# Second mixer: the low parts of its 32 weight tiles subtracted on VectorE instead of GpSimd

## The reference

```python
z = rmsnorm(x) @ w_in + b_in         # conv_a, conv_gate, q, k, v, o, i, f
u = conv_a * sigmoid(conv_gate)
u = silu(layernorm(causal_depthwise_conv(u, conv_w, conv_b)))      # 31 taps, 512 channels
qk = silu(causal_depthwise_conv([q, k], qk_conv_w, qk_conv_b))     # 4 taps
h = mlstm_chunkwise(q, k, v, i, f)                                 # 4 heads of 128
hm = groupnorm(sigmoid(o) * h) * mlstm_norm_g
x = x + [u, hm] @ w_out
```

## Time and profile before

| what | us |
|---|---|
| runs | 2023.34, 2024.51, 2026.22 |
| median | 2024.51 |
| profiled execution, span from first to last instruction | 2015.6 |
| median above that span | 8.9 |
| second mixer, first tile to end of tile 31 | 1182 to 1459 |
| expert stage | about 1493 to 1990 |

### The profile page before, as it was taken

One profiled execution on the slowest core, in us unless ns is written; L12 is line 12 of the kernel. 1 busy time (PEld: TensorE's weight loads), 2 busy tenths in 40 slices (PEclk: granted clock), 3 DMA queues, 4 the chain that ended last, 5 costly groups with the idle time before them and its releaser, 6 DMA issues.

```text
span 2015.6 us, 27480 instructions
## 1 busy us (share of the span) xinstructions
PE 1816.0 (90%) x9716; PEld 1274.7 (63%) x9716; DVE 852.1 (42%) x1244; ACT 436.7 (22%) x809; POOL 992.8 (49%) x536
## 2 busy tenths in 40 slices
PE   5999999999999799999999979998968988869783
PEld 4888888887777577888888747765743333323331
DVE  5444434320253567544443389777341111111114
ACT  3111100100244432111110053552321111111112
POOL 5888887777544378888887623321211111101001
PEclk8999999999999999999999989989979988989886
DMA  3333372433211123333333212210589999999995
GB/s 128 94 96 102 94 273 94 143 95 95 72 56 52 41 84 94 94 94 97 101 107 99 77 54 73 65 61 21 206 311 357 378 404 406 413 415 407 410 398 205
DMA packets 56977, 346.00 MB, mean 172 GB/s; under 512 B 8474, under 2 KB 8858, under 8 KB 44896
## 3 DMA queue, kind: packets, MB, share of 16 engines
q1 hardware_dynamic: 44640, 315.12, 42.7%
q10 hardware_dynamic: 7968, 19.46, 2.6%
q0 software_dynamic: 4320, 10.78, 1.5%
HBM read 475.06 MB, written 19.66 MB: 245 GB/s over the span
## 4 chain that ended last, share of the span: by engine, by line
PE 71%; DMA 14%; DVE 10%; ACT 3%; issue 1%; POOL 1%; SPq 0%; DVEq 0%; ACTq 0%; POOLq 0%
PE bank L460 31%; PE bank L431 12%; DMA big<-w_up_in 10%; PE bank L1821 7%; PE bank L1320 4%; PE bank L694 4%; PE bank L1839 2%; DVE big L1046 2%; PE bank L479 2%; PE bank L1434 2%; DMA ring<-w_down_in 1%; PE bank L1847 1%; DMA state<-w_down_in 1%; PE bank L612 1%; PE bank L672 1%
## 5 line engine op out<-in xcount | busy, mean ns | idle before, releaser
L277 POOL TENSOR_TENSOR weights_hi_parts<-ring,ones 128x1024 fp32r<-128x1024 f32 (+1 forms) x176 | 356.6, 2026 | 293.8 <-PE bank L460 130.2
L279 POOL TENSOR_TENSOR ring_parts<-ring,weights_hi_parts 128x1024 fp32r<-128x1024 f32 (+1 forms) x176 | 474.0, 2693 | 13.8
L460 PE MATMUL bank<-attention_buffers_parts,weights_hi_parts 128*128 128x512 f32 x832 | 328.1, 394 | 22.6 <-POOL ring_parts L279 17.9
L460 PE MATMUL bank<-state_parts,weights_hi_parts 128*128 128x512 f32 x832 | 325.7, 391 | 0.0
L460 PE MATMUL bank<-attention_buffers_parts,ring_parts 128*128 128x512 f32 x832 | 325.4, 391 | 0.0
L1821 PE MATMUL bank<-big,work 128*32 128x512 f32 x1440 | 227.6, 676 | 51.3 <-DMA big<-w_up_in 51.2
L431 PE MATMUL bank<-big_parts,weights_hi_parts 128*128 128x512 f32 x704 | 216.9, 389 | 1.2 <-POOL ring_parts L279 1.2
L460 PEld LDWEIGHTS bank<-attention_buffers_parts,weights_hi_parts 128*128 128x128 f32 x832 | 157.4, 189 | 59.1 <-POOL ring_parts L279 17.9
L1921 POOL TENSOR_TENSOR small<-small 128x1 f32<-128x1 f32 x51 | 9.7, 190 | 371.5 <-DVE small L1744 371.5
L866 POOL TENSOR_TENSOR ring_parts<-ring,weights_hi_parts 128x1024 fp32r<-128x1024 f32 x32 | 80.7, 2524 | 220.2 <-ACT weights_hi_parts L863 220.2
L460 PEld LDWEIGHTS bank<-state_parts,weights_hi_parts 128*128 128x128 f32 x832 | 157.5, 189 | 32.9 <-issue 0.8
(11 more groups left out here) (386 smaller groups left out, 2830.2 us busy)
## 6 DMA issues: line engine op xcount, KB each, us to landing
big<-w_up_in SPq DMA_DIRECT2D x54, 2048.0 KB
ring<-wdense_in SPq DMA_DIRECT2D x176, 512.0 KB, 3.6
state<-w_down_in SPq DMA_DIRECT2D x37, 2048.0 KB
big<-w_gate_in SPq DMA_DIRECT2D x36, 2048.0 KB
attention_buffers<-w_gate_in SPq DMA_DIRECT2D x18, 2048.0 KB
ring<-w_down_in SPq DMA_DIRECT2D x18, 2048.0 KB
ring<-wff_in SPq DMA_DIRECT2D x32, 704.0 KB, 4.1
y_rows<-big ACTq DMA_DIRECT2D x1, 8192.0 KB, 28.1
```

Source lines behind the costliest of these rows:

```text
L277: po.tensor_tensor(hi, raw, ones[:, 0:1].to_broadcast([128, words]), ALU.mult).then_inc(PO.sem, 1)
L279: po.tensor_tensor(lo, raw, hi.bitcast(F32), ALU.subtract) \
L460: m = pe.matmul(out, x, y_, start=j + n == 0, stop=j == len(pairs) - 1 and n == len(ts) - 1)
```

## The change

The low part of every tile of the second mixer is subtracted on VectorE, behind the same wait for the high part, and the planner's clock of VectorE is moved on by 1.15 for it. Nothing is left on GpSimd in the mixer.

```diff
             AC.wait(ring_freed[n - 2] if n >= 2 else before_ring[n + 2])
             hi_made[n] = AC.step(ac.activation(hi, raw, ACT.Copy))
             est("ac", 1.15)
-            PO.wait(hi_made[n])
-            lo_made[n] = PO.step(po.tensor_tensor(lo, raw, hi.bitcast(F32), ALU.subtract))
+            DV.wait(hi_made[n])
+            lo_made[n] = DV.step(dv.tensor_tensor(lo, raw, hi.bitcast(F32), ALU.subtract))
+            est("dv", 1.15)
```

## The result

| | median of runs, us | ratio to before, 95% interval |
|---|---|---|
| before | 2024.9 (2023.34 to 2026.22) | |
| changed | 2058.55 (2057.55 to 2062.05) | 1.0176 [1.0163, 1.0188] |

The change costs 33.65 us (before is now the median of four runs, one more than ahead of the prediction). Its sign and its place, the mixer's tail, were forecast; its size (22.7 us) was not, and 2058.55 lies outside the range of 2033 to 2056.

The account below looks back on a forecast made before the run. TensorE was taken to bound the mixer, DMA the expert stage. The tail's 28.4 us growth less 5.7 gained before it gives 22.7; span 2038.3 plus 8.9 gives 2047 us. Own range 2040 to 2055; 8 in 10, 2033 to 2056.

Parts of the forecast that it names:

- the mixer's tail: From X to the end of tile 29: 28 taps stand behind tile 27's waiting subtract, so it grows by 28.4 us.
- X: The end of head 3's last L315 in the mixer, forecast at 1399.5 us against 1405.2 before.
- The estimate of 1.2 us: One 128x1024 subtract on VectorE, estimated from nearest rows, with ends of 0.68 and 2.41 us.
- the load: VectorE in the mixer: 34 us of stalls removed against 38 us of subtracts added, so its load hardly changes.
- rival 2: VectorE's balance: gets 34 us back, pays 38, else nothing changes: +4 us, or 2027 if some is hidden; chance 0.05.
- Rival 1: Relief pays in full: TensorE never waits ahead of X, which comes 24.7 us earlier; net +0.3, 2025 us; chance 0.07.
- end of tile 24: End of the first output tile in the mixer, forecast at 1386.1 us against 1390.0 before.
- from there to X: From tile 24's end to head 3's last L315: a chain of high part, subtract, taps, reciprocal and others, 13.4 us.
- X to end of tile 29: The tail's length, forecast 69.3 us against 40.9 before.
- the middle: Mixer to tile 24's end: TensorE's losses sum to 11.3 us instead of 17.8, with 2.6 more work; uncertain by +-4.
- the start: First two subtracts stand ahead of the first reciprocal, so TensorE starts the mixer 1.9 us later.
- Rival 3: Clock and coupling cost more: half clock in the tail (+4 us), no gain before X (+6): 2057 us; chance 0.12.

Follow-up runs that it names:

- e12: Changed kernel with VectorE's subtract of tile 27 moved behind the 28 taps and the centring, just ahead of tile 28's subtract: 2046.9 us.
- e4: Changed kernel with no subtract on any engine in the mixer, the charge of 1.15 us and so its order kept: 2027.2 us.
- e19: Changed kernel with the planner counting 0.60 us for a tap, not 0.85, which puts all taps and the first sum ahead of tile 25: 2035.2 us.
- e2: Changed kernel without the planner's charge: subtract on VectorE, all else in the order of before: 2025.7 us.
- e3: Changed kernel with no subtract on any engine in the mixer and no charge, so the order of before: 2001.4 us.
- e1: Kernel before, subtract still on GpSimd, but the planner charges VectorE 1.15 us for it, giving the changed kernel's order: 2040.3 us.
- e10: Changed kernel with the subtracts of tiles 0 to 26 back on GpSimd, 27 to 31 on VectorE, order and charge kept: 2047.6 us.
- e16: Changed kernel with tile 25's high part on ScalarE behind the Exp that frees bank 1, its low part behind four later VectorE instructions: 2055.9 us.
- e8: Changed kernel with taps counted as 0.67 us, the subtract charged and issued 2.5 us of planner's TensorE clock behind its high part: 2031.9 us.
- e11: Changed kernel with the subtract uncharged and issued 4.0 us of planner's TensorE clock behind its high part: 2005.9 us.
- e15: Changed kernel with the subtract uncharged and issued 5.5 us of planner's TensorE clock behind its high part: 2008.4 us.
- e20: Changed kernel with taps counted as 0.60 us, the subtract charged and issued 4.0 us of planner's TensorE clock behind its high part: 2011.9 us.
- e5: Changed kernel with the subtract uncharged and issued 2.5 us of planner's TensorE clock behind its high part: 2011.0 us.
- e6: Changed kernel with the subtracts of tiles 27 to 31 back on GpSimd, order and charge kept: 2047.6 us.
- e7: Changed kernel with the planner counting 0.67 us for a tap, not 0.85; 2 taps stand behind head 3 instead of 28: 2043.4 us.
- e9: Changed kernel, charge and taps at 0.85 us kept, with the subtract issued 2.5 us of planner's TensorE clock behind its high part: 2045.1 us.
- e13: Changed kernel with only tiles 0 to 15 charged 1.15 us; 19 taps stand behind tile 27's subtract instead of 28: 2053.7 us.
- e18: Changed kernel with taps counted as 0.67 us and tile 27's subtract moved behind the last 2 taps and the centring: 2041.8 us.

## Why the prediction was right and wrong

**Right: the mechanism of the tail.** 28 taps behind head 3, behind a subtract that waits for tile 25. The wait was 8.56 us (over 6 forecast), the taps began at X + 9.7. e12 shows that the wait is on the path; e4, with the order and no subtract, and e19, with the charge and the sums put early, show that the place of taps and sums makes most of the rest. The estimate of 1.2 us held (1.225), and so did the load: 34 us of stalls went, 39.1 came, and where nothing else changed (e2) this gave +2.9 us; rival 2 had 4. Rival 1 took relief in full as 24.7 us; e3, without any subtract, gains 21.4.

**Wrong: the size.** The span after is 2057.2, forecast 2038.3. The 18.9 us, in the prediction's own terms:

| step | forecast | trace | over by |
|---|---|---|---|
| ahead of the mixer | as before | 1.5 later | 1.5 |
| end of tile 24 | 1386.1 | 1396.1, less 1.5 | 8.5 |
| from there to X | 13.4 | 13.6 | 0.2 |
| X to end of tile 29 | 69.3 | 73.3 | 4.0 |
| on to the expert stage | 47.7 | 51.2 | 3.5 |
| expert stage to the end | 521.6 | 523.0 | 1.4 |

(The last column adds up to 19.1 by rounding.)

The step that failed is **the middle, "these losses ... sum 11.3"**, from which "5.7 us gained" at X followed. I had TensorE at the end of tile 24 3.9 us earlier than before; by its column in the table of runs it came 4.5 later. Beside the 1.9 at the start I had 7.5 us of TensorE's idling in the sum; the first four stages above have 10.7 (lengths minus busy). I had 1.9 us of low clock; the stages have 0.03 x 58 + 0.04 x 80 + 0.04 x 45 = 6.7. Together 8.0 of the 8.5, and the larger part, 4.8, is clock. I had charged the waits by their length, and a low clock behind one of them only. In the changed kernel the granted clock was 0.83 from 1200 to 1210 us, behind the wait at L992 that I had foreseen, 0.66 from 1280 to 1290, behind the one at L1147, and 0.91 from 1320 to 1340. Of the waits, L992 came as walked and the one for L1379 is gone; missing were L1147 (2.15) and L1199 (3.72), while tile 22 waited only 0.7 instead of 2.7. Both missed ones are for bank 1, which in this code is freed by a reader (`one_read`), an instruction of VectorE or ScalarE; my walk followed operands and left out who frees the bank. The first is VectorE's: it is gone in e1. The second is the order's: e1 and e10 have it in full, and the high part queued ahead of the reader makes about 1 us of it (e16). What VectorE's subtract costs the middle, against GpSimd's in the same order, is 7.0 us by e1's column and 8.1 by e10's.

**The tail, 4.0 over.** Tile 25 took 7.4 (7.2 forecast), taps and L1098 1.0 more than forecast, since the last ten, all of one chunk, took 0.78 us each, the 18 ahead of them 0.67; behind that come small differences up to X + 59.4 for X + 56.6, and tiles 28 and 29 13.9 instead of 12.7.

**Rival 3** (chance 0.12) had 2057: +4 in the tail and +6 ahead of X. Measured +4.0 and, ahead of X, 8.7. Its number for the tail came true by luck: the places that it named, the second L460 group, tile 26's last bank and tile 27, ran at a granted clock of 1.00 (1446 to 1461.5 us). Its other half, no gain ahead of X, was the better account, and I gave it a small chance, because I took my walk's middle for known to +-4 us; it rested on one pass that could only find the waits I thought of. The range should have reached above rival 3.

**The two traces differ by 41.6 us, the times by 33.65.** The profiled execution of before was a quick one: its span lies 9.3 us under the median of 2024.9, whereas in the changed kernel and the other runs the time of an execution is 1.2 to 1.3 us over its span (2058.48 and 2057.2 for the changed kernel). So about 8 us of the traces' difference aren't the change's. The forecast was counted from that quick trace, and its median added the trace's 8.9 us as if they were a fixed gap. Counted in times, the miss is 33.65 - 22.7 = 11 us and not 18.9. Of the 8 us, the table above has 1.5 ahead of the mixer and 1.4 in the expert stage; where the rest lies no trace shows. Some may lie in the middle, since e2's column is 4.9 us over before's up to tile 24 while its time is 2.9 over, so the 8.5 there may be too much. The comparison of the changed kernel with e1 and e10 (7.0 and 8.1) doesn't use that trace. Only differences of times measure the change.

## What to carry to other kernels

When an instruction moves to an in-order engine, look first at what it waits for, not at how long it takes: here the same 32 subtracts, moved from GpSimd to VectorE, cost 3 us or 18 us by what stood behind them, and issued 4 us later by the plan's clock they made the kernel 17 us faster than with GpSimd. A wait on TensorE is to be priced with the low clock behind it, not by its length alone. A number in a planner's cost table is a change of its own and is tested by itself; here it carried more than the engine. In a walk of waits, list for each buffer or bank who frees it, not only who fills it.

## What the runs showed of the hardware that I had not expected

- The rule that I cited, that a GpSimd instruction and a two-input VectorE instruction in SBUF exclude each other (the Trainium skill, "SBUF — State Buffer", section "Who interferes with whom"), can be read off means in the run that has the new order and GpSimd (e1): L1047 takes 911 ns there, against 745 in the changed kernel, and L1032 1148 against 745. Of the 34 us of stalls at most two thirds were on the path, since leaving the subtract out gave 21.4 us.
- The same subtract of 128x1024 takes 2.41 us on GpSimd and 1.225 on VectorE.
- The router stage, from tile 29's end to the first matmul of the experts, has two lengths in the traces, 47.4 to 47.7 us (before, e2, e3, e4, e8, e11, e12, e15, e19, e20) or 50.8 to 51.5 (changed, e1, e5, e6, e7, e9, e10, e13, e16, e18). In the long ones the granted clock from 12 to 18 us behind tile 29 was 0.78 to 0.83, in the short ones 1.00, and matmuls run at half the rate for a while; the same eight transposes, of the changed kernel and of e12:

```profile
1499.15 1.95 PE L1511 MATMUL bank<-ident,big 128*128 128x128 f32 x8
```

```profile
1491.84 1.07 PE L1519 MATMUL bank<-ident,big 128*128 128x128 f32 x8
```

  Idling before it doesn't sort the kernels: e4 idles in the tail and is short, e5 doesn't and is long. What decides it stays open, and, with one trace of each kernel, also whether it goes with the kernel or with the execution; and with it 3.5 us of this change's price.
